# A hybrid decoder trunk on one core: where the last unit of keys is kept, and when the output weights are split

## What is computed

```python
qkv = (x @ w_qkv).reshape(bn, s, 3, B_HEADS, B_HEAD_DIM)      # 16 heads of 64
z = jnp.einsum('bthd,bshd->bhts', qb, kb).astype(jnp.float32) * scale
log_keep = jnp.where(causal, jax.nn.log_sigmoid(-z), 0.0)
survive = lax.cumsum(log_keep, axis=log_keep.ndim - 1, reverse=True) - log_keep
log_a = jax.nn.log_sigmoid(z) + survive
a = jnp.where(causal, jnp.exp(log_a), 0.0)
outs.append(jnp.einsum('bhts,bshd->bthd', a.astype(vb.dtype), vb))
...
return o @ w_out
```

## Time and profile before

| | |
|---|---|
| median of 3 runs | 2625.97 us (2625.22 to 2626.76) |
| the profiled execution | 2628.5 us |
| its span, first to last instruction | 2626.8 us |
| mean granted TensorE clock | 0.986 of full speed |
| busy: PE, PEld | 2523.3 us (96%), 2143.9 us (82%) |
| busy: DVE, POOL, ACT | 1484.2 (57%), 1112.9 (42%), 1031.3 us (39%) |
| DMA | 342.56 MB, mean 130 GB/s |
| attention, first score to start of the output projection | 1540.9 to 1870.3 us |

### The profile page before, as it was taken

How to read it: one execution, slowest core, us unless ns; L and a number is a source line. 1 busy time by engine, 2 the same in 40 slices (tenths; PEclk the granted TensorE clock), 3 DMA queues, 4 the chain that set the end, 5 groups by cost and what they waited for, 6 DMA issues and landing times.

```text
span 2626.8 us, 35467 instructions
## 1 busy us (share of the span) xinstructions
PE 2523.3 (96%) x13100; PEld 2143.9 (82%) x13100; DVE 1484.2 (57%) x1959; ACT 1031.3 (39%) x1507; POOL 1112.9 (42%) x716
## 2 busy tenths in 40 slices
PE   7999999997999999998999988999998999999997
PEld 7998888886888887887898867787896888888886
DVE  3215655658655588776511135666347655588775
ACT  5223212235444443334311147878344444443332
POOL 2221221236555546556222225545245555556554
PEclk9999999999999999999999989999998999999999
DMA  5223112132444564354323625444132444554443
GB/s 169 87 89 113 65 54 75 64 109 86 169 154 152 169 220 169 121 174 153 121 97 144 192 91 141 113 111 104 63 104 80 161 156 153 204 205 167 142 159 117
DMA packets 180417, 342.56 MB, mean 130 GB/s; under 512 B 12224, under 2 KB 95168, under 8 KB 178240
## 3 DMA queue, kind: packets, MB, share of 16 engines
q1 hardware_dynamic: 173632, 311.47, 36.6%
q10 hardware_dynamic: 6656, 29.36, 2.8%
HBM read 235.95 MB, written 104.86 MB: 130 GB/s over the span
## 4 chain that ended last, share of the span: by engine, by line
PE 79%; DVE 7%; ACT 4%; issue 4%; DMA 3%; POOL 2%; SPq 0%; DVEq 0%; ACTq 0%; POOLq 0%
PE psum L1171 22%; PE psum L1217 18%; PE psum L986 13%; PE psum L973 13%; PE psum L997 4%; PE psum L1307 3%; PE psum L1294 2%; PE psum L1277 2%; DVE stick L2201 1%; PE psum L1090 1%; POOL rw_lo L927 1%; DMA a_raw<-a_forms 1%; ACT brk L1697 1%; DVE ra_lo L2081 1%; ACT psum L1703 1%
## 5 line engine op out<-in xcount | busy, mean ns | idle before, releaser
L1217 PE MATMUL psum<-rw_hi,ra_hi 128*128 128x512 f32 x896 | 352.9, 394 | 19.3 <-DVE acc L2099 15.0
L1217 PE MATMUL psum<-rw_lo,ra_hi 128*128 128x512 f32 x896 | 351.1, 392 | 0.0
L1217 PE MATMUL psum<-rw_hi,ra_lo 128*128 128x512 f32 x896 | 350.7, 391 | 0.0
L830 POOL TENSOR_TENSOR w_lo<-stage,w_hi 128x1024 fp32r<-128x1024 f32 x56 | 134.0, 2415 | 493.2 <-ACT w_hi L1373 493.2
L927 POOL TENSOR_TENSOR rw_lo<-blk,rw_hi 128x512 fp32r<-128x512 f32 x152 | 231.7, 1554 | 185.2 <-ACT rw_hi L1520 185.2
L2201 DVE TENSOR_TENSOR_SCAN stick<-psum,brk 128x128 f32<-128x128 f32 (+7 forms) x128 | 172.6, 1354 | 125.7 <-ACT psum L1703 125.2
L1509 ACT ACTIVATE ra_hi<-a_raw 128x2048 fp32r<-128x2048 f32 x56 | 107.4, 1917 | 341.4 <-PE psum L1217 227.5
L2081 DVE TENSOR_TENSOR ra_lo<-a_raw,ra_hi 128x512 fp32r<-128x512 f32 x224 | 226.0, 1017 | 25.4 <-ACT ra_hi L1509 25.3
L946 POOL TENSOR_TENSOR brk<-brk,stick 128x128 f32<-128x128 f32 (+7 forms) x128 | 152.9, 1206 | 189.9 <-DVE stick L2201 177.3
L986 PE MATMUL psum<-w_hi,hT_hi 128*128 128x256 f32 x768 | 218.7, 285 | 2.5 <-DVE hT_lo L2208 1.4
L1217 PEld LDWEIGHTS psum<-rw_hi,ra_hi 128*128 128x128 f32 x896 | 169.5, 189 | 59.3 <-issue 16.3
(11 more groups left out here) (229 smaller groups left out, 6424.0 us busy)
## 6 DMA issues: line engine op xcount, KB each, us to landing
a_raw<-a_forms SPq DMA_DIRECT2D x56, 1024.0 KB, 6.1
a_forms<-a_out SPq DMA_DIRECT2D x64, 512.0 KB, 3.1
blk<-mlp_w_in SPq DMA_DIRECT2D x28, 1024.0 KB, 5.4
a_forms<-a_out SPq DMA_DIRECT2D x32, 768.0 KB, 3.3
stage<-a_w_in_in SPq DMA_DIRECT2D x16, 1024.0 KB, 5.4
stage<-mlp_w_in SPq DMA_DIRECT2D x16, 1024.0 KB, 6.0
raw<-mlp_w_in SPq DMA_DIRECT2D x32, 512.0 KB, 5.5
x_res<-xt SPq DMA_DIRECT2D x24, 512.0 KB, 4.8
```

The costliest lines, as they stand in the source:

```text
L830: pool.tensor_tensor(w[b][1][:, c], raw[:, c], w[b][0][:, c].bitcast(F32), ALU.subtract).then_inc(unit_ready, 1)
L1217: mm = pe.matmul(psum[:, down_bank(n, tp), :], ring_a[n % 3][sa][:, k, tp * P:(tp + 1) * P], ring_w[n % 3][sw][:, k, :], start=(p in (1, 2 ...
```

## The change

- Two buffers `a_last` (high and low part) are laid over `stage_q` and the high part of `wq[0]`, which are done with by then. The last unit of keys is rounded and stored from there, not from `a_buf[1]`. So ACT and DVE, in the first pair, wait only for the third of the four stores from `a_buf[1]`.
- `U_O` is still loaded at the same place. Its high part is now made in two halves, after steps 4 and 5 of the first pair; its low part in four quarters on POOL in the last pair, after tiles 1, 2 and (two) 3.
- `U_O + 1` is loaded after the q, k and v of all heads; its high part follows step 7 of the last pair on ACT, its low part all of POOL's tiles. `U_O + 2` is loaded after the four tiles of x.
- POOL's loop now takes pairs 0 to 6, and the last pair is written out. DVE's loop over the query and key units has its last turn written out.

```diff
@@ -354,6 +354,8 @@
         stage_q = kb("stage_q", [P, US], F32, 160)
         wq = [[kb(f"wq{b}_{s}", [P, US], F32R, k + 8 * n) for n, s in enumerate(("hi", "lo"))]
               for b, k in enumerate((168, 0))]
+
+        a_last = [kb("a_last_hi", [P, 2, TOK], F32R, 160), kb("a_last_lo", [P, 2, TOK], F32R, 168)]
         H = [{p: [kb(f"h{layer}_{p}{s}", [P, 4, HALF], F32R, k + 8 * n) for n, s in enumerate(("hi", "lo"))]
@@ -782,22 +784,22 @@
                 load_v(0, h)
             sp.wait_ge(front_psum, FI_O)
             unit(U_O, cols(w_bout, 0), stage_c)
-            unit(U_O + 1, cols(w_bout, 1), stage_c)
             for b in range(2):
                 wait(sp, qk_out[b], 32 * (2 * D // UC) // 2)
             for b in range(2):
                 load_qk(2 + b, b)
                 load_v(1, b)
-            unit(U_O + 2, cols(w_bout, 2), stage_c)
             with sp.Fori(2, HEADS // 2) as i:
                 for b in range(2):
                     load_qk(2 * i + b, b)
                     load_v(i, b)
+            unit(U_O + 1, cols(w_bout, 1), stage_c)
             wait(sp, o_split, 2 * HEADS)
             load_g(3)
             for t in range(4):
                 load_x(3, t)
+            unit(U_O + 2, cols(w_bout, 2), stage_c)
             unit(U_O + 3, cols(w_bout, 3), stage_c)
             wait(sp, unit_ready, U_END * 2)
             load_up(1, 0)
@@ -946,14 +948,26 @@
                 pool.tensor_tensor(brk[m][e][:, c0:c1], brk[m][e][:, c0:c1], stick[m][e][:, c0 + 1:c1 + 1],
                                    ALU.mult).then_inc(a_done, 1)
-            for k in range(2 * NT):
-                stick_mult(k, 0)
-                if k in (7, 11):
-                    lo(U_O + (k - 7) // 4, (k - 7) // 4)
-            with pool.Fori(1, HEADS // 2) as i:
+            def lo_quarter(n, q):
+
+                c = slice(q * (US // 4), (q + 1) * (US // 4))
+                pool.wait_ge(unit_hi, n + 1)
+                ins = pool.tensor_tensor(wt[0][1][:, c], stage[:, c], wt[0][0][:, c].bitcast(F32), ALU.subtract)
+                if q % 2:
+                    ins.then_inc(unit_ready, 1)
+
+            with pool.Fori(0, HEADS // 2 - 1) as i:
                 for k in range(2 * NT):
                     stick_mult(k, i * (2 * NT))
-            for n in range(U_O + 2, U_END):
+            for k in range(2 * NT):
+                stick_mult(k, (HEADS // 2 - 1) * (2 * NT))
+                if k in (1, 2):
+                    lo_quarter(U_O, k - 1)
+                if k == 3:
+                    lo_quarter(U_O, 2)
+                    lo_quarter(U_O, 3)
+            pool.wait_ge(qk_out[1], 32 * (2 * D // UC) // 2)
+            for n in range(U_O + 1, U_END):
                 lo(n, n % 2)
             mlp_boundary(3, 1)
             add_x(4, 0, 2)
@@ -1371,6 +1385,14 @@
                 act.wait_ge(unit_landed, n * 16 + 16)
                 act.activation(w[b][0][:], raw[:], ACT.Copy).then_inc(unit_hi, 1)
+
+            def hi_half(n, h):
+
+                cols_ = slice(h * (US // 2), (h + 1) * (US // 2))
+                act.wait_ge(unit_landed, n * 16 + 16)
+                ins = act.activation(wt[0][0][:, cols_], stage[:, cols_], ACT.Copy)
+                if h:
+                    ins.then_inc(unit_hi, 1)
             def square_m(b, t):
                 n = NT * (b - 1) + t
@@ -1669,16 +1691,17 @@
                 for b in range(2):
                     if not (isinstance(i, int) and i == 0):
                         act.wait_ge(qk_out[b], i * 32)
+                    dst = a_last if last and b else a_buf[b]
                     for j in range(4):
                         act.wait_ge(front_psum, i * 8 + (FI_QK + 4 * b + j + 1))
-                        act.activation(a_buf[b][0][:, j % 2, (j // 2) * HALF:(j // 2 + 1) * HALF], psum[:, j, :],
+                        act.activation(dst[0][:, j % 2, (j // 2) * HALF:(j // 2 + 1) * HALF], psum[:, j, :],
                                        ACT.Copy).then_inc(front_hi, 1)
                     if not last:
                         hi(i * 2 + (U_QK + b + 2), b, wq, stage_q)
                     act.wait_ge(dve_evac, i * 8 + (FI_QK - FI_V2 + 4 * b + 4))
                     for s in range(2):
                         act.dma_start(qk_dram[s].rearrange("(u p) n -> p u n", p=P)[:, bass.ds(4 * i + 2 * b, 2), :].bitcast(F32),
-                                      a_buf[b][s][:].bitcast(F32)).then_inc(qk_out[b], 16)
+                                      dst[s][:].bitcast(F32)).then_inc(qk_out[b], 16)
             qk_step(0)
             with act.Fori(1, D // UC - 1) as i:
                 qk_step(i)
@@ -1724,7 +1747,7 @@
                     for k in range(4):
                         break_tile(0, k)
                         keep_tile(0, k)
-                    act.wait_ge(qk_out[1], 32 * (2 * D // UC) // 2)
+                    act.wait_ge(qk_out[1], 32 * ((2 * D // UC) // 2 - 1))
                 for n in range(2 * QP):
                     out = None if n % 2 == 0 or (first and n == 1) else (i, n // 2 - 1) if n > 1 else (i - 1, 3)
@@ -1745,8 +1768,10 @@
                         keep_tile(i, 2 * n + 5)
                     if here > 3:
                         keys_in(i, n, 3)
-                    if first and n in (2, 4):
-                        hi(U_O + n // 2 - 1, n // 2 - 1)
+                    if first and n in (4, 5):
+                        hi_half(U_O, n - 4)
+                    if last and n == 2 * QP - 1:
+                        hi(U_O + 1, 1)
             iterate(act, HEADS // 2, att_step)
             out_hi(HEADS // 2 - 1, 3)
@@ -2167,13 +2192,18 @@
                         dve.wait_ge(front_psum, FI_V2 + t + HALF_T + 1)
                     dve.tensor_copy(v2ring[b][:, :, t, :, :],
                                     psum[:, t % 4, c0:c0 + UC].rearrange("p (h s d) -> p h s d", h=2, s=2)).then_inc(dve_evac, 1)
-            with dve.Fori(0, D // UC) as i:
+            def qk_lo(i, last=False):
                 for b in range(2):
+                    buf = a_last if last and b else a_buf[b]
                     for j in range(4):
                         dst = (slice(None), j % 2, slice((j // 2) * HALF, (j // 2 + 1) * HALF))
                         dve.wait_ge(front_hi, i * 8 + (hi_count[0] + 4 * b + j + 1))
-                        ins = dve.tensor_tensor(a_buf[b][1][dst], psum[:, j, :], a_buf[b][0][dst].bitcast(F32), ALU.subtract)
+                        ins = dve.tensor_tensor(buf[1][dst], psum[:, j, :], buf[0][dst].bitcast(F32), ALU.subtract)
                         ins.then_inc(dve_evac, 1)
+
+            with dve.Fori(0, D // UC - 1) as i:
+                qk_lo(i)
+            qk_lo(D // UC - 1, last=True)
             hi_count[0] += 4 * 2 * D // UC
@@ -2213,7 +2243,7 @@
                 if first:
                     for k in range(4):
                         sticks(0, k)
-                    dve.wait_ge(qk_out[1], 32 * (2 * D // UC) // 2)
+                    dve.wait_ge(qk_out[1], 32 * ((2 * D // UC) // 2 - 1))
                     ones_column(QP - 1)
                     dve.wait_ge(rows_set, 2 + 2 * QP)
                 for n in range(2 * QP):
```

## The result

The changed kernel takes 2613.82 us (median of 5 runs, 2612.22 to 2615.19) against 2625.97 of the kernel before; the ratio is 0.995, 95% interval 0.9939 to 0.996. In later runs, with 9 of the kernel before beside them, it was 2614.52 against 2627.66, ratio 0.9947 (0.9933 to 0.9961). So it is faster by 12 to 13 us. The profiled execution took 2615.19 us with a span of 2613.5, against 2628.5 and 2626.8: 13.3 us by the profile.

What follows compares the result with a forecast made beforehand. PE was taken as the bound, with waits and half clock in the first pair. Gains 5.2 + 0.4 + 7.9 less 0.1 made 13.4 us, forecasting 2612.6 us against the median of 2625.97; range 2609 to 2618.

Steps and rivals of the forecast that it cites:

- step 1: First pair's ramp: tile 4 stops waiting for the last key store, full clock returns sooner; 5.2 us gained at tile 7.
- step 2: First head, tile 7 to tile 12: the first split leaves; gain 0.4 us, bounds 0 and 1.9.
- step 3: Second head: second split and late keys leave, two halves of the first high part come in; net gain 7.9 us.
- step 4: Last pair: four quarters on POOL and later loads of output units; cost 0.1 us, bounds 0 and 2.
- The rival in which the keys stay late: Second head: keys of head 2 still late, or clock still falls; 5.3 us less gain, 2617.9 us; chance 0.07.
- The rule weighed: VectorE and GpSimd's shared SBUF port lock: DVE's scan, one input in PSUM, is not held up by POOL's low part.
- the lock: Rival, last pair: POOL's quarters and DVE's scans block each other; 4.6 us, 2617.2 us; chance 0.03.
- the last rounding: Rival, attention's end: U_O + 1 lands late, holding ACT before its last rounding; 2631 us and up; chance 0.02.
- More than the steady part gives: Rival, first two heads: clock hardly falls in the ramp and they wait less than steady ones; about 2610 us; chance 0.06.

Runs made afterwards that it cites:

- the table edit: Changed kernel with the sigmoid table loaded before the last two units of keys; 2611.44 us, ratio 0.9935 to the kernel before.

## Why the prediction was right, step by step

The forecast was 2612.6 us and a gain of 13.4; measured were 2613.82, 12.2 below the median of before, and 13.3 by the profile. The parts were less right than the sum: by the first profile step 1 gave 0.9 us less than forecast, step 2 0.4, step 3 0.2 and step 4 0.1 more. That they nearly cancel is luck.

**Step 1** (5.2 us at tile 7): 4.3 in the first profile (tile 7's sigmoid 15.72 us behind the first score, was 20.02), 4.9 in the second. The term that was too large is PE's start on tile 6: counted from the first score it came 3.1 us earlier in the first profile and 3.9 in the second, where I had 4.06. I had tile 4 start at once behind tile 3, since its scores had been ready; in the first profile they ran at half clock themselves, 1.83 us where they had taken 1.05, and ACT waited 0.91 us for them; in the second they took 1.05 and ACT did not wait. The full clock came back near 1554.6 us, 0.9 later than the 1553.7 I had.

**Step 2** (0.4): tile 7 to tile 12 went from 11.54 to 10.77 us, 0.8. I had taken the second pair's 11.17 as the floor, and the first pair runs below it without the split. With the first split in its old place the two kernels without a second split stay at 11.54, keys late or early, so the split's price is 0.8 and not 0.4. Why a first head is shorter there than a steady one, no run shows.

**Step 3** (7.9): 27.44 to 19.34 is 8.1 us. The size was right, the reason incomplete. I read the 5.26 us before tile 0 as the late keys' price, called the order of loads "the second thing the change removes", and added the split to it as if they followed one another. The runs show them in parallel: the order alone gains nothing, the late split alone next to nothing (26.96 to 26.51), both together 7 to 8 us. It came out right only because the change makes both edits. The rival in which the keys stay late had 5.3 us less gain; by the runs it would have been 6.8 (323.43 less 316.62, two kernels that differ in the order of the loads alone). For the halves I had 0.3 us; 19.34 against 19.24 of a steady head gives 0.1, though each took 1.05 us and not 0.96.

**Step 4** (0.1): 0.0. The rest of the attention took 269.69 us against 269.66. `U_O + 1` and `U_O + 2` took 7.6 and 11.4 us to land, longer than my 5.9 and 10, far from mattering: the latter was there at 1871.5 and taken at 1880.1. The quarters took 1.26 to 1.29 us each, not 1.16.

**The rule weighed.** The scan of 896 keys started in the middle of the third quarter, at 1818.57 us, and took 2.02 us, the mean of such scans without one; the scan of 384 keys beside the first quarter took 0.96 us, as in the kernel before. So the wording of the Trainium skill, SBUF — State Buffer, "SBUF: two separate sides", by which VectorE needs two SBUF inputs or a 2-port mode to meet GpSimd, is the one that the trace agrees with here; the shorter one of its "Terms" would have made the first of these scans wait.

The rivals: neither the lock nor the last rounding showed. *More than the steady part gives* did not come with this change, but its reason, a clock that hardly falls in the ramp, is what the one profile of the table edit shows.

## What to carry to other kernels

A row that says "idle, released by X" names the last of the things waited for, not the only one. Before pricing an edit that removes X, list what else was late in the same stretch (here POOL, whose product of tile 12 stood 8 us late behind a low part, at a row PE had not come to yet) and ask when PE would have gone on without X. A queue in order holds up what stands behind a wait: SP's second load held back the keys, and POOL's second low part, waiting for that same unit, held back the products. A rounding cut in two halves that fit ACT's gaps cost about 0.1 us where the whole one cost 0.8 more, but four quarters of a low part earned only 0.3 us over one run of 5 us. A buffer that frees an engine from a store also frees the moment at which the store is issued.

## What I had not expected of the hardware

The ramp of one and the same kernel has two lengths, 5.63 and 6.47 us to tile 4, in the eight profiles of kernels with the buffer and this ramp, each length in four of them: PE's clock falls to 1.2 GHz either before or after tile 4's scores (1.05 or 1.83 us long), after the same wait of 2.4 us. In one of them, late keys without the second split, it also came back in between (1.00 from 1548 to 1550 us) and fell again (0.57 over the next 4). And in the one profile with the table loaded early it did not fall at all, in a stretch 2.1 to 2.7 us shorter for 1.28 us of table; how often that happens stays open.
